# Gate and up projections: three matmuls of 256 columns a weight block against one of 512 and one of 256, with an addition on VectorE

## The chip, the cores and the metric

The kernel runs on one core of a Trainium2 chip. The metric is device microseconds of that core for one execution, 985.59 us as the median of three runs (983.49 to 986.75). The profile is one further execution of the same program.

## The reference, cut to what matters

Two transformer-like blocks run over 256 tokens of width 1024, in float32. The change touches the first half of both feed-forward parts:

```python
# first block
h = rmsnorm(x, ffn_pre_norm)
f = (silu(h @ w_ffn_gate) * (h @ w_ffn_up)) @ w_ffn_down
# second block: w_up has 2 * 2816 columns
u = h @ w_up
u = sum(pad(u)[:, j:j + t] * conv_w[j] for j in range(3)) + conv_b
a, g = split(u, 2)
f = (gelu(a) * g) @ w_down
```

d_ff is 2816, so that each of the two stages makes 22 pairs of output tiles of 128 features by 256 tokens, with 8 weight blocks of 128x128 to each tile.

## The kernel before, in words

**Numbers in two parts.** Every float32 operand of a projection is split into a high part (a cast to fp32r) and a low part (the value minus the high part). A product is three matmuls: high weight by high activation, high weight by low activation, low weight by high activation (PASSES, line 1488).

**The weight stream.** All weights come as one stream of 128x128 blocks. SP loads slots of 16 blocks (1 MB) into `raw`, which has three slots (line 477); before slot n it waits until the low parts of slot n-3 are made. Eight blocks are a unit. ScalarE casts a unit to `w_hi` (line 582), after PE has finished the unit four before. The low part `w_lo` of a unit is made by VectorE (line 975, even units) or GpSimd (line 545, odd units) as a tensor_tensor with `raw` and `w_hi` as inputs; in the first two fills of the gate and of the up stage VectorE makes all of them (`_DVE_ONLY`, line 90). PE waits for the low part at the first block of each unit (line 1496).

**A fill.** `pair` (line 1527) fills one PSUM bank of the ring `pj` (three banks): two tiles of 256 columns, 8 blocks each, 3 matmuls a block, so 48 matmuls and two units. The stages in question are `ff` (22 fills of gate and up of the first block) and `up` (22 fills of the second). `pe_step` counts finished fills and units.

**What follows a fill.** The engines run in the order of the program. For `ff` fill j, ScalarE: cast of unit 2j+4 (`split_target`, possible from the middle of the fill), wait for the end of the fill, cast of unit 2j+5 (`behind_target`), silu of the gate half (line 759), then the high part of product j-1 (line 762). VectorE: low part of unit 2j+4 (`feed_behind`, line 1201), product with the other half (line 1205), then the low part of product j-1 (`ff_lo`, line 1194). For `up` fill j, ScalarE: the two casts in the same way, two activations (line 929), gelu of j-1 (line 935), high part of product j-2 (line 938). VectorE: low part of unit 2j+4, wait for line 929, four scalar_tensor_tensor for the convolution (lines 1456 and 1463, one input in PSUM and one in SBUF), `ff_lo` of j-2 (line 1194), product of j-1 (line 1473, both inputs in SBUF). GpSimd makes the low part of unit 2j+5.

**What comes next.** `stream("down")` and `stream("down2")` (line 1570) take the activations `ff` as the stationary operand and four weight blocks (512 columns) as the moving one, into `acc` (four banks).

**Memory.** In SBUF, in this order: `raw` (24 KiB of each partition), `w_hi` and `w_lo` (16 KiB each), `x`, `y`, `sq` (8 KiB each), `h` (16 KiB, from 80 to 96 KiB, all high parts ahead of all low parts), constants and small buffers, and from about 120 KiB the arena, in which buffers of different stages share places: `ff` from its start (44 KiB), `merged_s` and `o_hg_s` at +32 KiB, `mix` at +35, `mem_n` at +51, `o_na` at +56, `o_ca` at +64. PSUM holds `pj` (banks 0 to 2), `acc` (3 to 6) and `st` (7).

Of the kernel before, what the change touches and what calls it, by code (L numbers as in the profile page):

```python
# [41 lines left out]
UB = 8  # L42
SBUF_WORDS = 52912
PJ = 3

# [22 lines left out]
RING = [n for n, f in enumerate(FILLS) if f[3] != "acc"]  # L68
INDEX = {(name, j): n for n, (name, j, _, _) in enumerate(FILLS)}
FIRST_BLOCK = [sum(f[2] for f in FILLS[:n]) for n in range(len(FILLS) + 1)]  # L70
NBLOCKS = FIRST_BLOCK[-1]
# [97 lines left out]
def program(nc, x_tok, mem_tok, pt, wstream, wproj, vecs, gains, consts, rope_tab, decay_tab, rpb, out, toep):  # L169
    ctx = ExitStack()  # L170
    with ctx:
# [18 lines left out]

        raw = place("raw", [RAW, 16, P])
        w_hi = place("w_hi", [UNITS, UB, P], R32)
        w_lo = place("w_lo", [UNITS, UB, P], R32)
        x = place("x", [2, D])
        y = place("y", [KT, S])
        sq = place("sq", [KT, S])
        h = place("h", [2, KT, S], R32)
        vec = place("vec", [NVEC])
# [11 lines left out]
        soft = place("soft", [2, 3, 2])  # L210
        arena = (top[0] + 127) // 128 * 128

        def at(kib, name, *shape, dt=F32):
            return place(name, list(shape), dt, offset=arena + int(1024 * kib))

# [55 lines left out]

        pj = [ctx.enter_context(nc.psum_tensor(f"pj{i}", [P, 2, S], F32)) for i in range(PJ)]
        acc = ctx.enter_context(nc.psum_tensor("acc", [P, 2, D], F32))
        sc = [acc[:, i // 2, 512 * (i % 2):512 * (i % 2) + 512] for i in range(4)]
        st = ctx.enter_context(nc.psum_tensor("st", [P, 512], F32))

# [19 lines left out]
        f_hi = sem("f_hi")  # L296
        up_full = sem("up_full")
        acc_done = sem("acc_done")
        mean_ready = sem("mean_ready")
# [75 lines left out]
        def bank(name, j):  # L375
            return pj[RING.index(fi(name, j)) % PJ]

# [191 lines left out]
        def _(act):  # L569
# [185 lines left out]
            for j in range(23):  # L755
                if j < 22:
                    wait_fill("ff", j)
                    wait_gate_slot(act, "ff", j)
                    A(gate_tmp[:, gate_slot("ff", j), 0], bank("ff", j)[:, 0], ACT.Silu).then_inc(gate_done, 1)  # L759
                if j:  # L760
                    wait_read(act, "ff", j - 1)
                    nc.scalar.copy(ff[:, 0, j - 1], prod_tmp[:, (j - 1) % 2]).then_inc(f_hi, 1)
# [160 lines left out]
            for j in range(24):  # L923
                if j < 22:
                    wait_fill("up", j)
                    if j >= 2:
                        act.wait_ge(up_full, j - 1)
                    for i in range(2):
                        ins = A(gate_tmp[:, j % 2, i], bank("up", j)[:, i], ACT.Identity,  # L929
                                bias=col("conv_b", 22 * i + j), scale=col("conv_w", 44 + 22 * i + j))  # L930
                    ins.then_inc(up_lin, 1)
# [14 lines left out]
        def _(dve):  # L946
# [248 lines left out]

            ff_lo.count = 0
            dve.wait_ge(toep_zero, 16)
            for j in range(23):
                if j < 22:
                    gates[0] += 1  # L1200
                    feed_behind("ff", j)
                    wait_gate(gates[0])
                    if j >= 2:
                        dve.wait_ge(ff_ready, j - 1)
                    V.tensor_tensor(prod_tmp[:, j % 2], bank("ff", j)[:, 1], gate_tmp[:, gate_slot("ff", j), 0],  # L1205
                                    ALU.mult).then_inc(freed["dve"], 1)
# [241 lines left out]
            for j in range(24):  # L1448
                if j < 22:
                    feed_behind("up", j)  # L1450
                    dve.wait_ge(up_lin, j + 1)
# [32 lines left out]
        def _(pe):  # L1484
# [21 lines left out]
            def open_fill(name, j):  # L1506
                n = fi(name, j)
                r = RING.index(n)
                if r >= PJ:
                    m = RING[r - PJ]  # L1510
                    who = FILLS[m][3]
                    pe.wait_ge(freed[who], freed_count(m, who))
                assert at_block[0] == FIRST_BLOCK[n] or FILLS[n][2] == 0
                return pj[r % PJ]

            def tile_out(dst, src, kts=KT, ready=None, turn=0):

                for n in range(kts):
# [4 lines left out]
                    for i, (a, b) in enumerate(PASSES):  # L1523
                        last = mm(dst, w[a], src[:, b, kt], start=n == 0 and i == 0, stop=n == kts - 1 and i == 2)  # L1524
                    step(last, at_block[0])

            def pair(name, j, src, kts=KT, ready=None, turn=0):
# [169 lines left out]
            for j in range(22):  # L1697
                pair("ff", j, h, ready=h_turned("wout"))

            def ff_kt(first):  # L1700
                def ready(i, tt):
                    if tt == 0:
                        pe.wait_ge(ff_ready, first + i + 1)
# [11 lines left out]

            stream("down", ff_part, FT, ff_kt(0), ahead_of={FT - 4 + 7: ("down", (0, 1))})
            stream("ple", h_part, KT, ple_ready, head=4, tail=2, ahead_of={3: ("down", (2, 3))})
# [180 lines left out]
            for j in range(22):  # L1898
                pair("up", j, h, ready=h_turned("wout2"))
            stream("down2", ff_part, FT, ff_kt(FT))  # L1900

# [123 lines left out]
```

## Time and profile before

| what | value |
|---|---|
| median of the runs | 985.59 us |
| the profiled execution, its own time | 984.05 us |
| its span, first to last instruction | 982.3 us |
| PE busy (matmul) | 947.2 us, 96% |
| weight loads busy | 888.0 us, 90% |
| VectorE, ScalarE, GpSimd busy | 624.7, 514.5, 325.7 us |
| share of PE in the chain that ended last | 83% |
| gate stage `ff`, first to last fill | 168.1 to 295.0 us |
| `up` stage | 785.3 to 913.7 us |
| granted TensorE clock, mean | 0.995 of 2.4 GHz |

The span is 1.75 us shorter than the execution's own time. Matmuls are pipelined and their ends are modelled, so the time of a run of matmuls is read from their starts, or from the chain of waits, and not from their busy time.

### The profile page before, as it was taken

How to read it: one execution, taken by the hardware profiler on the slowest of the kernel's cores; microseconds unless marked ns; L12 is line 12 of the kernel's file. 1: busy time of each engine (PE TensorE's matmuls, PEld its weight loads, DVE VectorE, ACT ScalarE, POOL GpSimd, SP SyncE). 2: the span in 40 equal slices, each digit the busy share in tenths (PEclk: the TensorE clock that was granted, in tenths of full speed). 3: DMA queues.
4: the chain of work that ended last, by engine and by line, in shares of the span. 5: the costliest groups of instructions: out<-in, count | busy, mean ns of one | idle time of the engine just before them, and what ended most of it. 6: DMA issues, size and time to landing. Idle time of an engine off the chain costs nothing.

```text
span 982.3 us, 16396 instructions
## 1 busy us (share of the span) xinstructions
PE 947.2 (96%) x6822; PEld 888.0 (90%) x6822; DVE 624.7 (64%) x842; ACT 514.5 (52%) x790; POOL 325.7 (33%) x136
## 2 busy tenths in 40 slices
PE   7999999999999999999999999999899899999997
PEld 7998986999998878999999998998799799999885
DVE  4998576566663257567598978865555545666522
ACT  6853475444444356555444445555445456666532
POOL 0000000334434400002564533555685124443441
PEclk9999999999999999999999999999999999999999
DMA  9652344655555454545524335333356445555551
GB/s 356 208 202 86 139 149 152 199 190 191 172 178 205 175 171 172 172 171 173 172 87 133 127 99 179 129 129 129 130 176 214 147 163 199 176 172 189 190 178 43
DMA packets 30441, 162.65 MB, mean 166 GB/s; under 512 B 9089, under 2 KB 9489, under 8 KB 11936
## 3 DMA queue, kind: packets, MB, share of 16 engines
q1 hardware_dynamic: 30304, 161.53, 48.1%
q8 instruction: 54, 0.88, 0.4%
q14 instruction: 19, 0.16, 0.0%
q0 software_dynamic: 64, 0.08, 0.0%
HBM read 160.48 MB, written 1.12 MB: 165 GB/s over the span
## 4 chain that ended last, share of the span: by engine, by line
PE 83%; DVE 9%; ACT 4%; issue 2%; DMA 2%; SPq 0%; DVEq 0%; ACTq 0%
PE pj L1524 52%; PE acc L1589 18%; PE pj L1542 5%; PE acc L1761 3%; DMA raw<-wstream 2%; PE acc L1624 1%; DVE w_lo L975 1%; ACT w_hi L582 1%; DVE y L1027 1%; ACT sq L588 1%; PE st L1624 1%; DVE ret_inv L1138 1%; DVE conv_y L1067 1%; PE acc L1838 0%; DVE h L1033 0%
## 5 line engine op out<-in xcount | busy, mean ns | idle before, releaser
L545 POOL TENSOR_TENSOR w_lo<-raw,w_hi 128x1024 fp32r<-128x1024 f32 x124 | 313.9, 2536 | 636.0 <-ACT w_hi L582 635.8
L1524 PE MATMUL pj<-h,w_hi 128*128 128x256 f32 x2816 | 512.3, 284 | 7.7 <-DVE h L1033 3.9
L582 ACT CAST w_hi<-raw 128x1024 fp32r<-128x1024 f32 x284 | 296.2, 1048 | 344.4 <-PE pj L1524 240.3
L1524 PEld LDWEIGHTS pj<-h,w_hi 128*128 128x128 f32 x2816 | 440.4, 192 | 11.1 <-issue 5.8
L1524 PE MATMUL pj<-h,w_lo 128*128 128x256 f32 x1408 | 399.0, 283 | 0.0
L975 DVE TENSOR_TENSOR w_lo<-raw,w_hi 128x1024 fp32r<-128x1024 f32 x160 | 201.8, 1270 | 126.2 <-ACT w_hi L582 116.1
L1524 PEld LDWEIGHTS pj<-h,w_lo 128*128 128x128 f32 x1408 | 270.8, 192 | 0.0
L1589 PE MATMUL acc<-w_hi,ff 128*128 128x512 f32 x352 | 96.1, 395 | 0.0
L1589 PEld LDWEIGHTS acc<-w_hi,ff 128*128 128x128 f32 x352 | 66.1, 188 | 15.2
L1589 PE MATMUL acc<-w_lo,ff 128*128 128x512 f32 x176 | 55.2, 395 | 0.0
L1194 DVE TENSOR_TENSOR ff<-prod_tmp,ff 128x256 fp32r<-128x256 f32 x44 | 53.6, 1221 | 0.9 <-ACT ff L938 0.9
L1456 DVE SCALAR_TENSOR_TENSOR gate_tmp<-pj,vec,gate_tmp 128x255 f32<-128x255 f32 x44 | 19.2, 478 | 48.3 <-ACT gate_tmp L929 48.3
L1542 PE MATMUL pj<-w_hi,h 128*128 128x256 f32 x256 | 46.9, 285 | 0.8 <-ACT v_ret L655 0.8
L1542 PEld LDWEIGHTS pj<-w_hi,h 128*128 128x128 f32 x256 | 40.0, 192 | 1.1 <-ACT v_ret L655 1.0
L1589 PEld LDWEIGHTS acc<-w_lo,ff 128*128 128x128 f32 x176 | 33.2, 188 | 7.7
L1205 DVE TENSOR_TENSOR prod_tmp<-pj,gate_tmp 128x256 f32<-128x256 f32 x22 | 9.3, 424 | 43.9 <-ACT gate_tmp L759 43.9
L1542 PE MATMUL pj<-w_lo,h 128*128 128x256 f32 x128 | 36.2, 283 | 0.0
L1290 DVE COPY_PREDICATED st_hg<-con,acc 128x256 f32<-128x256 int32 x56 | 21.9, 444 | 15.5 <-PE acc L1761 13.8
L1067 DVE SCALAR_TENSOR_TENSOR conv_y<-conv_in,vec,conv_y 128x256 f32<-128x256 f32 x74 | 31.2, 479 | 0.5
L1418 DVE TENSOR_TENSOR merged<-merged,prod_tmp 128x256 f32<-128x256 f32 x16 | 26.2, 1641 | 0.5
L1542 PEld LDWEIGHTS pj<-w_lo,h 128*128 128x128 f32 x128 | 24.5, 192 | 0.0
L1413 DVE SCALAR_TENSOR_TENSOR prod_tmp<-gate_tmp,pj 128x256 f32<-128x256 f32 x16 | 6.7, 420 | 26.5 <-ACT gate_tmp L907 26.5
(241 smaller groups left out, 1159.2 us busy)
## 6 DMA issues: line engine op xcount, KB each, us to landing
raw<-wstream SPq DMA_DIRECT2D x142, 1024.0 KB, 4.9
toep_t<-toep SPq DMA_DIRECT2D x16, 96.0 KB, 3.0
x<-x_tok SPq DMA_DIRECT2D x2, 512.0 KB, 5.0
mem<-mem_tok SPq DMA_DIRECT2D x1, 1024.0 KB, 12.1
w_ple<-wproj SPq DMA_DIRECT2D x1, 1024.0 KB, 7.1
out_t<-y SPq DMA_DIRECT2D x4, 256.0 KB, 2.3
decay<-decay_tab SPq DMA_DIRECT2D x1, 768.0 KB, 5.8
gain_mix_pre<-gains SPq DMA_DIRECT2D x1, 512.0 KB, 6.5
```

Source lines behind the costliest of these rows:

```text
L545: nc.gpsimd.tensor_tensor(w_lo[:, u % UNITS], unit_of_raw(u), as_f32(w_hi[:, u % UNITS]), ALU.subtract).then_inc(lo_ready["pool"], 1)
L582: nc.scalar.copy(w_hi[:, u % UNITS], unit_of_raw(u)).then_inc(hi_ready, 1)
L975: V.tensor_tensor(w_lo[:, u % UNITS], unit_of_raw(u), as_f32(w_hi[:, u % UNITS]), ALU.subtract).then_inc(lo_ready["dve"], 1)
L1067: ins = V.scalar_tensor_tensor(out=conv_y[:, j], in0=src, scalar=weight, in1=conv_y[:, j], op0=ALU.mult, op1=ALU.add)
L1194: V.tensor_tensor(ff[:, 1, j], prod_tmp[:, j % 2], as_f32(ff[:, 0, j]), ALU.subtract).then_inc(ff_ready, 1)
L1290: ins = V.copy_predicated(dst[:, 4 * a:4 * a + 4:3], m2, src)
L1418: ins = V.tensor_tensor(merged[:, j], merged[:, j], prod_tmp[:, i % 2], ALU.add)
L1524: last = mm(dst, w[a], src[:, b, kt], start=n == 0 and i == 0, stop=n == kts - 1 and i == 2)
L1542: last = mm(b[:, tt], src[:, xa, kt, tt * P:tt * P + P], ws[kt][wa], start=kt == 0 and i == 0, stop=kt == KT - 1 and i == 2)
L1589: last = mm(acc[:, tt, 512 * g:512 * g + 512], src(b, i, tt), w[:, u % UNITS, 4 * g:4 * g + 4].rearrange("p a b -> p (a b)"), start=i == 0 ...
L1624: last = mm(out, diag[:, w], conv_in[:, t, w:w + S], start=w == first, stop=w == end - 1)
L1761: last = mm(sc[g][:, c:c + P], tile(k_mix[g // 2], 2 * (g % 2) + a, tt), q, start=True, stop=True)
```

## The change

The two stages use a new helper `wide_pair`. For each weight block it issues one matmul of the high weight against high and low activations side by side (512 columns, into a whole bank) and one of the low weight against the high activations (256 columns, added to the first half of that bank). A fill now takes two banks, one for each tile, and alternates between banks 6, 7 (half of `acc`) and 0, 1. After the fill VectorE adds the two halves of both banks with one tensor_reduce over 128x1024 values into one bank (3 for even fills, 2 for odd), which the consumers then read. ScalarE waits for that sum.

```diff
+WIDE_BANKS = ((6, 7), (0, 1))
+SUM_BANKS = (PJ, 2)
...
-        raw = place("raw", [RAW, 16, P])
         w_hi = place("w_hi", [UNITS, UB, P], R32)
         w_lo = place("w_lo", [UNITS, UB, P], R32)
+        h_both = place("h", [KT, 2, S], R32)
+        h = h_both[:].rearrange("p k b s -> p b k s")
+        arena = (top[0] + 127) // 128 * 128
+        top[0] = arena + 1024 * ARENA_KIB
+        raw = place("raw", [RAW, 16, P])
         x = place("x", [2, D])
...
-        h = place("h", [2, KT, S], R32)
...
+        ring = ctx.enter_context(nc.psum_tensor("ring", [P, PJ + 1, 2, S], F32))
+        pj = [ring[:, i] for i in range(PJ)]
+        st = ring[:, PJ].rearrange("p a s -> p (a s)")
...
# ScalarE, in both stages
                 if j < 22:
                     wait_fill("ff", j)
+                    wait_summed(act, "ff", j)
...
# VectorE
+            def add_halves(name, j):
+                dve.wait_ge(pe_step, fill_step(fi(name, j)))
+                b = wide(name, j)
+                V.tensor_reduce(bank(name, j), b.rearrange("p i a s -> p i s a"), AX.X, ALU.add).then_inc(summed, 1)
...
+                    add_halves("ff", j)
                     feed_behind("ff", j)
...
+                    add_halves("up", j)
                     feed_behind("up", j)
...
# PE
             def open_fill(name, j):
                 n = fi(name, j)
-                r = RING.index(n)
-                if r >= PJ:
-                    m = RING[r - PJ]
-                    who = FILLS[m][3]
-                    pe.wait_ge(freed[who], freed_count(m, who))
+                for m in earlier_fills(n):
+                    if name in WIDE and FILLS[m][0] == name:
+                        wait_summed(pe, *FILLS[m][:2])
+                    else:
+                        pe.wait_ge(freed[FILLS[m][3]], freed_count(m, FILLS[m][3]))
...
+            def wide_pair(name, j, ready):
+                b = open_fill(name, j)
+                for i in range(2):
+                    both = b[:, i].rearrange("p a s -> p (a s)")
+                    for kt in range(KT):
+                        w = take()
+                        if i == 0 and j == 0:
+                            ready(kt)
+                        mm(both, w[0], h_both[:, kt].rearrange("p a s -> p (a s)"), start=kt == 0, stop=False)
+                        last = mm(b[:, i, 0], w[1], h[:, 0, kt], start=False, stop=kt == KT - 1)
+                        step(last, at_block[0])
...
             for j in range(22):
-                pair("ff", j, h, ready=h_turned("wout"))
+                wide_pair("ff", j, h_turned("wout"))
...
             for j in range(22):
-                pair("up", j, h, ready=h_turned("wout2"))
+                wide_pair("up", j, h_turned("wout2"))
```

`earlier_fills` names the last fills that used the same banks; within a stage PE waits before fill j for the sum of fill j-2. The down projections wait for the sum of fill 20 before they write the banks 6 and 7. In the new layout `w_hi`, `w_lo` and `h` lie below 48 KiB, the arena from 48 to 132 KiB, `raw` and the rest above it.

## Rows read from the trace of the kernel before

**Rows 1.** The page: busy time by engine, and the chain that ended last
```profile
PE 947.2 (96%) x6822; PEld 888.0 (90%) x6822; DVE 624.7 (64%) x842; ACT 514.5 (52%) x790; POOL 325.7 (33%) x136
...
PE 83%; DVE 9%; ACT 4%; issue 2%; DMA 2%; SPq 0%; DVEq 0%; ACTq 0%
PE pj L1524 52%; PE acc L1589 18%; PE pj L1542 5%; PE acc L1761 3%; DMA raw<-wstream 2%; PE acc L1624 1%; DVE w_lo L975 1%; ACT w_hi L582 1%; DVE y L1027 1%; ACT sq L588 1%; PE st L1624 1%; DVE ret_inv L1138 1%; DVE conv_y L1067 1%; PE acc L1838 0%; DVE h L1033 0%
```

**Rows 2.** The chain in order of time (start us, us, what, how many)
```profile
168.09 126.94 PE pj L1524 x1056
...
754.58 16.74 PE acc L1589 x72
785.31 128.44 PE pj L1524 x1056
913.75 61.35 PE acc L1589 x264
```

**Rows 3.** Busy time by stage: gate stage, then up stage
```profile
168.10:295.00 126.90, 126.90 (x1057) 126.90 (x1058) 76.70 (x64) 58.30 (x85) 50.48 (x21) 1.00 0.56 189
...
790.00:912.00 122.00, 122.00 (x1019) 122.00 (x1018) 73.31 (x143) 77.41 (x125) 50.79 (x21) 1.00 0.53 181
```

**Rows 4.** The chain from 368 to 378 us: `h` stationary, 512 moving columns
```profile
367.86 10.20 PE acc L1589 x45
```

**Rows 5.** VectorE's groups by shape, whole span
```profile
L1360 DVE TENSOR_REDUCE soft<-acc 128x2 f32<-128x512 f32 x4 | 2.7, 682 | 0.0
...
L1479 DVE TENSOR_TENSOR x<-x,acc 128x1024 f32<-128x1024 f32 x2 | 2.4, 1221 | 7.1 <-PE acc L1589 7.1
```

**Rows 6.** One up fill in order of time: last matmul, ScalarE's cast, VectorE, GpSimd
```profile
850.11 0.28 PE L1524 MATMUL pj<-h,w_lo 128*128 128x256 f32 x1
...
850.48 1.05 ACT L582 CAST w_hi<-raw 128x1024 fp32r<-128x1024 f32 x1 [1.83 <-PE pj L1524]
...
851.43 1.01 ACT L929 ACTIVATE gate_tmp<-pj,vec 128x256 f32<-128x256 f32 x2
851.61 2.42 POOL L545 TENSOR_TENSOR w_lo<-raw,w_hi 128x1024 fp32r<-128x1024 f32 x1 [3.34 <-ACT w_hi L582]
852.35 0.41 ACT L935 ACTIVATE gate_tmp<-gate_tmp 128x256 f32<-128x256 f32 x1
852.48 0.87 DVE L1456 SCALAR_TENSOR_TENSOR gate_tmp<-pj,vec,gate_tmp 128x255 f32<-128x255 f32 x2 [2.17 <-ACT gate_tmp L929]
852.65 0.40 ACT L938 CAST ff<-prod_tmp 128x256 fp32r<-128x256 f32 x1
...
854.18 0.41 DVE L1194 TENSOR_TENSOR ff<-prod_tmp,ff 128x256 fp32r<-128x256 f32 x1
854.51 0.42 DVE L1473 TENSOR_TENSOR prod_tmp<-gate_tmp 128x256 f32<-128x256 f32 x1
854.85 1.22 DVE L975 TENSOR_TENSOR w_lo<-raw,w_hi 128x1024 fp32r<-128x1024 f32 x1
```

**Rows 7.** One gate fill in order of time: GpSimd and VectorE
```profile
198.33 2.40 POOL L545 TENSOR_TENSOR w_lo<-raw,w_hi 128x1024 fp32r<-128x1024 f32 x1 [3.35 <-ACT w_hi L582]
198.57 0.42 DVE L1205 TENSOR_TENSOR prod_tmp<-pj,gate_tmp 128x256 f32<-128x256 f32 x1 [1.94 <-ACT gate_tmp L759]
198.91 2.10 DVE L1194 TENSOR_TENSOR ff<-prod_tmp,ff 128x256 fp32r<-128x256 f32 x1
```

**Rows 8.** Down projection in order of time: VectorE, then GpSimd
```profile
924.35 2.67 DVE L975 TENSOR_TENSOR w_lo<-raw,w_hi 128x1024 fp32r<-128x1024 f32 x1 [0.68 <-ACT w_hi L582]
...
926.07 3.22 POOL L545 TENSOR_TENSOR w_lo<-raw,w_hi 128x1024 fp32r<-128x1024 f32 x1
```

**Rows 9.** Near-simultaneous starts, in order of time: GpSimd, then VectorE
```profile
610.10 2.90 POOL L545 TENSOR_TENSOR w_lo<-raw,w_hi 128x1024 fp32r<-128x1024 f32 x1 [0.48 <-ACT w_hi L582]
...
610.10 0.68 DVE L989 TENSOR_TENSOR o_hg_s<-o_hg,o_hg_s 128x512 fp32r<-128x512 f32 x1
```

**Rows 10.** DMA: the weight slots, KB each, median us to landing
```profile
raw<-wstream SPq DMA_DIRECT2D x142, 1024.0 KB, 4.9
```

More of the change, by code:

```diff
@@ L43 @@
 SBUF_WORDS = 52912
+ARENA_KIB = 84
 PJ = 3
@@ L69, with filled_banks, read_banks, earlier_fills @@
 INDEX = {(name, j): n for n, (name, j, _, _) in enumerate(FILLS)}
+WIDE = ("ff", "up")
+WIDE_FILLS = [(name, j) for name, j, _, _ in FILLS if name in WIDE]
+WIDE_BANKS = ((6, 7), (0, 1))
+SUM_BANKS = (PJ, 2)
+def filled_banks(n):
+    name, j = FILLS[n][:2]
+    return WIDE_BANKS[j % 2] if name in WIDE else (RING.index(n) % PJ,)
+def read_banks(n):
+    name, j = FILLS[n][:2]
+    return (SUM_BANKS[j % 2],) if name in WIDE else filled_banks(n)
+def earlier_fills(n):
+    found = set()
+    for b in filled_banks(n):
+        before = [m for m in RING if m < n and b in filled_banks(m) + read_banks(m)]
+        found.update(before[-1:])
+    return sorted(found)
 FIRST_BLOCK = [sum(f[2] for f in FILLS[:n]) for n in range(len(FILLS) + 1)]
@@ L210, in program @@
         soft = place("soft", [2, 3, 2])
-        arena = (top[0] + 127) // 128 * 128
         def at(kib, name, *shape, dt=F32):
+            assert 1024 * kib + 4 * np.prod(shape) <= 1024 * ARENA_KIB, name
             return place(name, list(shape), dt, offset=arena + int(1024 * kib))
@@ L270, in program @@
         squares = gate_tmp[:].rearrange("p a b s -> p (a b s)")
-        pj = [ctx.enter_context(nc.psum_tensor(f"pj{i}", [P, 2, S], F32)) for i in range(PJ)]
+        ring = ctx.enter_context(nc.psum_tensor("ring", [P, PJ + 1, 2, S], F32))
+        pj = [ring[:, i] for i in range(PJ)]
+        st = ring[:, PJ].rearrange("p a s -> p (a s)")
         acc = ctx.enter_context(nc.psum_tensor("acc", [P, 2, D], F32))
+        acc4 = acc[:].rearrange("p t (b a s) -> p (t b) a s", b=2, a=2)
         sc = [acc[:, i // 2, 512 * (i % 2):512 * (i % 2) + 512] for i in range(4)]
-        st = ctx.enter_context(nc.psum_tensor("st", [P, 512], F32))
         mix_keys = sem("mix_keys")
@@ L297, in program @@
         up_full = sem("up_full")
+        summed = sem("summed")
         acc_done = sem("acc_done")
@@ L375, in bank, with wide, wait_summed @@
         def bank(name, j):
-            return pj[RING.index(fi(name, j)) % PJ]
+            return ring[:, read_banks(fi(name, j))[0]]
+        def wide(name, j):
+            a, b = filled_banks(fi(name, j))
+            return acc4[:, 2:4] if a == 6 else ring[:, a:b + 1]
+        def wait_summed(eng, name, j):
+            eng.wait_ge(summed, WIDE_FILLS.index((name, j)) + 1)
         def flat(b):
@@ L925, in _ @@
                     wait_fill("up", j)
+                    wait_summed(act, "up", j)
                     if j >= 2:
@@ L1507, in open_fill @@
                 n = fi(name, j)
-                r = RING.index(n)
-                if r >= PJ:
-                    m = RING[r - PJ]
-                    who = FILLS[m][3]
-                    pe.wait_ge(freed[who], freed_count(m, who))
+                for m in earlier_fills(n):
[3 more added lines that the diff above has]
+                        pe.wait_ge(freed[FILLS[m][3]], freed_count(m, FILLS[m][3]))
                 assert at_block[0] == FIRST_BLOCK[n] or FILLS[n][2] == 0
-                return pj[r % PJ]
+                return wide(name, j) if name in WIDE else pj[filled_banks(n)[0]]
             def tile_out(dst, src, kts=KT, ready=None, turn=0):
@@ L1697, in _, with ff_kt @@
             for j in range(22):
-                pair("ff", j, h, ready=h_turned("wout"))
-            def ff_kt(first):
+                wide_pair("ff", j, h_turned("wout"))
+            def ff_kt(first, wide_name):
                 def ready(i, tt):
+                    if i == 0 and tt == 1:
+                        wait_summed(pe, wide_name, 20)
                     if tt == 0:
@@ L1714, in ple_ready @@
                     wait_turned("down", 2 * tt + i // 4)
-            stream("down", ff_part, FT, ff_kt(0), ahead_of={FT - 4 + 7: ("down", (0, 1))})
+            stream("down", ff_part, FT, ff_kt(0, "ff"), ahead_of={FT - 4 + 7: ("down", (0, 1))})
             stream("ple", h_part, KT, ple_ready, head=4, tail=2, ahead_of={3: ("down", (2, 3))})
@@ L1898, in _ @@
             for j in range(22):
-                pair("up", j, h, ready=h_turned("wout2"))
-            stream("down2", ff_part, FT, ff_kt(FT))
+                wide_pair("up", j, h_turned("wout2"))
+            stream("down2", ff_part, FT, ff_kt(FT, "up"))
 def host_layout(inputs):
```

## The prediction

> **What bounds the kernel now.** I read the page first, for the engine that is full: PE is busy 96% of the span and carries 83% of the chain; the pairs' line 1524 alone has 52% [rows 1]. Then the chain in order of time: the gate stage is one unbroken piece of 126.94 us for its 1,056 matmuls, and the up stage one of 128.44 us [rows 2]. So both stages go at PE's pace: 126.94 / 1,056 = 120.2 ns a matmul, 5.77 us a fill (5.76 in steady state). The up stage is longer by 1.5 us; the change doesn't touch that. Third, the stage table: VectorE is busy 76.7 of 126.9 us in the gate stage and 73.3 of 122 us in the up stage [rows 3], that is 3.5 and 3.5 us of each 5.76 us fill. PE sets the time, and VectorE has 2.3 us to spare in each fill. The argument turns on whether the new addition fits there, and on when.
>
> **Part 1, the matmuls.** Each block loses two matmuls of 256 columns and gains one of 512. 256 columns take 120 ns where 2.4 GHz (granted clock 1.00 in both stages [rows 3]) needs 106.7: 13.3 ns for each matmul beside its columns. For 512 columns there are three rows: 45 in 10.20 us = 226.7 ns with `h` stationary [rows 4], 264 in 61.35 us = 232.4 ns with `ff`, and 72 in 16.74 us = 232.5 ns with `merged_s` [rows 2]. The nearest is 226.7, since it has the weights and `h` as operands and is again 13.3 ns over its columns. So a block costs 226.7 + 120 = 346.7 instead of 360 ns: 13.3 ns for 352 blocks = 4.7 us a stage, **9.4 us** in both; a fill takes 5.55 us. Bounds: at 240 ns (two matmuls of 256, nothing shared) the gain is 0; at 232.4 it is 5.4 us; at the bare 213.3 ns it is 18.8 us.
>
> The Trainium skill (TensorE: Matmul & The Clock Gate, Back-to-back issue gap) puts an isolated matmul at columns / 2.4 GHz + 2.5 ns. By that a block would go from 327.6 to 325.0 ns, and the change would bring 1.8 us in all. The 120 ns of this trace disagree with its 109, so the sum goes by the rows.
>
> **Part 2, the layout.** Streams whose activation buffer lies at 120 KiB and above take 232.4 ns, the one with `h` (80 to 96 KiB) 226.7 [rows 2, 4]. After the change `ff` lies at 48 to 92 KiB and `merged_s` at 80 to 96. If the place is the cause, 528 + 96 matmuls gain 5.7 ns each, 3.6 us; I take **3.1 us**, since nothing in the trace separates place from buffer and part of the other buffers moves too. Ends: 0 and 4 us. The move of `raw` to 132 KiB I cost at nothing: the slots land in 4.9 us [rows 10], less than a fill, and are needed over a fill later.
>
> **Part 3, the addition.** 44 tensor_reduce of 1,024 inputs and 512 outputs on VectorE. The nearest row has 512 inputs from PSUM, 682 ns; a 1,024 tensor_tensor with PSUM input takes 1,221 [rows 5]. 682 + 512 / 0.96 GHz = 1.22 us. Half as much isn't excluded by a row but would need two inputs a cycle; the upper end is 2.1 us, one more pass for the 512 outputs. 44 x 1.22 = 54 us of VectorE, all beside PE if the order works out.
>
> **Part 4, the order on VectorE.** Count from the start of the cast of the odd unit, which the end of a fill releases [rows 6] (at 850.48, 0.37 after the start of the last matmul). GpSimd's low part starts at 1.13 and ends at 3.55 [rows 6]. A VectorE instruction with two SBUF inputs and a GpSimd low part exclude each other: the 256-element `ff_lo` that started 0.58 after GpSimd took 2.10 instead of 0.41 us and ended 0.28 after it [rows 7, 6]; a low part that met GpSimd took 2.67, and GpSimd behind it 3.22 instead of 2.40 [rows 8, 7]. Instructions with one input in PSUM run through (0.42 during GpSimd [rows 7]; lines 1456 and 1463 alike [rows 6]).
>
> Now the addition comes first: 0 to 1.22. Behind it on VectorE stands the even unit's low part, made until now in mid-fill, when GpSimd was done. It starts at about 1.16 (successors start 0.07 early [rows 6]), against GpSimd's 1.13. **This is a race within 0.03 us.** At a tie in the trace VectorE got through (0.68 us) and GpSimd took 2.90 [rows 9]; at +0.58 it lost [rows 7].
>
> *VectorE first:* its low part ends at 2.4, GpSimd's at 4.65. In the up stage ScalarE waits for the sum until 1.25, its two activations end at 2.3, the convolution runs 2.3 to 4.0, `ff_lo` is blocked until 4.9, the product ends at 5.3: before the next fill's end at 5.55, with 0.3 to spare. PE needs the even low part at 5.55 and the odd one at 8.3. Nothing stalls. In the gate stage the work ends at 4.9.
>
> *GpSimd first:* the low part ends at 3.55 + 1.08 = 4.63. Gate stage: product and `ff_lo` until 5.3, still inside the fill, so 4.7 us are gained either way. Up stage: four convolution steps (1.70), `ff_lo` (0.33) and product (0.33 + 0.08) [rows 6] end at 7.0, past 5.55, see the first rival.
>
> PE waits for the sum of two fills before, at least 3 us old in either case. The DMA of a slot starts up to 1.3 us later and has over 3 us of slack. At the end of the gate stage the last high part comes some 4 us later on ScalarE (the addition, then a product behind a late low part), and with it the cast of the fifth unit of the down projection; that unit is needed 11 us after the stage, so it costs nothing.
>
> **Sum.** 984.05 (the profiled execution; span 982.3) - 9.4 - 3.1 = 971.6. The median is 1.54 above that execution, so 973.1: **973 us**.
>
> **Rivals.**
>
> *A. GpSimd wins the race, and the up stage falls behind: slower.* The product (two SBUF inputs) starts at 6.59, which is 1.04 of the next fill, 0.09 ahead of GpSimd's 1.13: GpSimd is held 0.19 (as rows 8 and 9 show), the low part ends 0.19 later, and a fill or two later the product comes behind GpSimd and is blocked itself. From then on PE waits for low parts. The loop over two fills: convolution, `ff_lo`, product 2.40; addition 1.21; ScalarE's activations, gelu, high part and two casts 2.67; GpSimd's start 1.13 and work 2.40; `ff_lo` and product behind it 0.27 + 0.28; addition 1.14; low part 1.22: 12.7 us for two fills, 6.36 each where 5.76 were. Five fills at 5.55 and sixteen at some 6.35 make +8.0 for the up stage, and the down projection after it starts on late low parts, +2.4. Sum: 984.05 - 4.7 + 8.0 + 2.4 - 3.1 = 986.7, or 988.2 against the median; each 0.1 us on the addition makes it 1.6 more. With 1.3 us, where GpSimd wins more surely, 989.7. It decides at an addition of some 1.2 us and ends at some 1.6, where the product falls behind GpSimd's end. For it: the arithmetic above. Against it: the tie of rows 9, and a race that I can't place to 0.03 us.
>
> The Trainium skill (SBUF — State Buffer, Who interferes with whom) has the same mechanism as a rule: a VectorE instruction with two SBUF inputs and a GpSimd one that reads SBUF share a port pair, and the one that issues first blocks the other for its whole length. Rows 7 and 8 agree. By "issues first" read to the letter, 1.13 is before 1.16 and rival A is the outcome.
>
> *B. The addition takes 1.6 to 2.1 us.* The up stage then has no blocked product but VectorE is nearly full: some 5.76 a fill, a gain of 1.9 less 1.2 of late low parts; 984.05 - 4.7 - 0.7 - 3.1 = 975.6, or 977 against the median. For it: strided reads from two banks and PSUM outputs, which no row shows.
>
> *C. The matmul of 512 gains nothing over two of 256* (the 13.3 ns go with the columns): only the layout's 3.1 is left, 982.5; and without that 985.6. Against it: rows 4. A milder case, 232.4 ns, gives 977.
>
> **Chances.** Forecast with VectorE first, 0.54; A 0.26; B 0.10; C 0.04; the milder case of C or something else in between 0.06. About 0.3%, 3 us, is what a measurement can tell from no change. A splits into 0.08 within 3 us and 0.18 above; C and a partial A give 0.07 more within; the others are faster: faster 0.66, same 0.15, slower 0.19. Range: the forecast with the layout's and the pitch's bounds reaches from 968 to 977, its own range; to leave out no more than 2 in 10 it has to reach through A: 968 to 989.5.
>
> **What would show it.** In the timeline of a gate fill: wide matmuls 227 ns apart to the next start, 5.55 us a fill, stage pieces of 122 and 124 us in the chain. TENSOR_REDUCE 128x512 at 1.22 us. In an up fill, VectorE's low part at 1.2 us when it won, above 3 us when it lost; the product at 0.42, or above 2 us in rival A, with PE waiting for `w_lo` of line 975. Down projections at 227 ns. The forecast is wrong if PE waits for VectorE in the up stage, if the addition is longer than 1.3 us, or if the 512 columns take over 232 ns.

## The result, and the profile after

| | before | changed |
|---|---|---|
| median of the runs | 986.17 us (983.49 to 987.03) | 976.36 us (973.71 to 977.04) |
| ratio to the kernel before | | 0.9906 (0.9889 to 0.9924) |
| the profiled execution | 984.05 us | 973.71 us |

The medians are of four executions each. Run again later on another occasion the changed kernel stood at 0.9917 (0.9891 to 0.9943). By these ratios it is 8 to 9 us faster (the two medians above are 9.8 apart). Forecast were 973 us and a gain of 12.5.

First the page of the changed kernel, its busy time and the shares of the chain:

```profile
PE 936.8 (96%) x6118; PEld 848.7 (87%) x6118; DVE 688.4 (71%) x886; ACT 518.2 (53%) x790; POOL 371.1 (38%) x136
...
PE 86%; DVE 8%; ACT 4%; issue 2%; DMA 1%; SPq 0%; DVEq 0%; ACTq 0%
PE ring L1579 28%; PE acc L1657 18%; PE acc L1591 9%; PE ring L1591 8%; PE ring L1610 5%; PE acc L1592 4%; PE ring L1592 4%; PE acc L1831 3%; PE acc L1692 1%; ACT w_hi L627 1%; DVE w_lo L1022 1%; DVE y L1074 1%; DMA gain_mix_pre<-gains 1%; PE ring L1692 1%; DVE ret_inv L1185 1%
```

PE has 704 instructions fewer and is still full. VectorE went up by 64 us and none of it shows: its share of the chain fell from 9 to 8% against [rows 1]. GpSimd's busy time rose by 45 us with the same 136 instructions; something holds it.

The chain in order of time (start us, us, what, how many), against [rows 2]:

```profile
291.78 58.54 PE acc L1657 x258
...
358.95 15.25 PE acc L1657 x66
...
750.47 19.08 PE acc L1657 x84
...
904.67 59.98 PE acc L1657 x264
```

The down projection of the second block takes 59.98 us for its 264 matmuls, 227.2 ns each (232.4 before), and starts at 904.67 instead of 913.75. At its end the changed kernel is 10.4 us ahead in these two executions, which both had a mean granted clock of 0.995.

The busy time by stage (gate, then up), against [rows 3]:

```profile
172.90:291.60 118.70, 118.70 (x674) 102.99 (x673) 100.82 (x83) 59.37 (x84) 72.23 (x21) 1.00 0.56 191
786.00:904.00 118.00, 118.00 (x682) 103.21 (x682) 107.65 (x164) 78.07 (x125) 72.47 (x21) 1.00 0.55 185
```

Each block has two matmuls now. The gate stage: 118.7 us / 674 x 2 = 352.2 ns a block; the up stage: 118.0 / 682 x 2 = 346.0. (A few matmul starts are rounded in at the edges; between the starts of two additions there are 5.65 us in the gate and 5.547 us in the up stage, 353 and 346.7 ns a block.) Before it was 360 ns in both. From its first matmul to the first of the down projection the gate stage took 124.4 us instead of 126.8, the up stage 123.7 instead of 128.3. So the up stage gained the forecast 4.7 us and the gate stage half of it. VectorE is 85% busy in the gate stage and 91% in the up stage.

One fill of the up stage in order of time (start us, us, engine, line, operation), against [rows 6]:

```profile
849.24 1.23 DVE L1248 TENSOR_REDUCE ring<-ring 128x512 f32<-128x1024 f32 x1 [0.30 <-PE ring L1592]
849.29 1.05 ACT L627 CAST w_hi<-raw 128x1024 fp32r<-128x1024 f32 x1 [1.72 <-PE ring L1592]
850.38 1.22 DVE L1022 TENSOR_TENSOR w_lo<-raw,w_hi 128x1024 fp32r<-128x1024 f32 x1
850.42 3.45 POOL L590 TENSOR_TENSOR w_lo<-raw,w_hi 128x1024 fp32r<-128x1024 f32 x1 [2.10 <-ACT w_hi L627]
850.51 1.02 ACT L976 ACTIVATE gate_tmp<-ring,vec 128x256 f32<-128x256 f32 x2 [0.16 <-DVE ring L1248]
...
851.56 0.87 DVE L1511 SCALAR_TENSOR_TENSOR gate_tmp<-ring,vec,gate_tmp 128x255 f32<-128x255 f32 x2
...
853.26 0.89 DVE L1241 TENSOR_TENSOR ff<-prod_tmp,ff 128x256 fp32r<-128x256 f32 x1
...
854.08 0.41 DVE L1528 TENSOR_TENSOR prod_tmp<-gate_tmp 128x256 f32<-128x256 f32 x1
854.78 1.23 DVE L1248 TENSOR_REDUCE ring<-acc 128x512 f32<-128x1024 f32 x1 [0.30 <-PE acc L1592]
```

The addition takes 1.23 us. VectorE's low part starts at 850.38 and runs 1.22 us undisturbed; GpSimd's starts 0.04 later and takes 3.45 us instead of 2.42. The race was won by 40 ns. That is where GpSimd's 45 us come from: 22 low parts in each stage, 44 times about 1.03. `ff_lo` is then held by GpSimd (0.89 instead of 0.41), the product ends at 854.49, and VectorE waits 0.30 us for the next fill to end. This 0.3 us a fill is all the slack that VectorE has left in the up stage.

### The profile page after: what moved, and what is told of

It is laid out like the page before. It is cut to its first block, busy times and chain, and to the rows that moved or that the text cites. A ratio compares the mean times of both kernels' runs of the same rounds, so it can differ in the third digit from the quotient of the medians.

```text
span 971.9 us, 15074 instructions
## 1 busy us (share of the span) xinstructions
PE 936.8 (96%) x6118; PEld 848.7 (87%) x6118; DVE 688.4 (71%) x886; ACT 518.2 (53%) x790; POOL 371.1 (38%) x136
## 4 chain that ended last, share of the span: by engine, by line
PE 86%; DVE 8%; ACT 4%; issue 2%; DMA 1%; SPq 0%; DVEq 0%; ACTq 0%
PE ring L1579 28%; PE acc L1657 18%; PE acc L1591 9%; PE ring L1591 8%; PE ring L1610 5%; PE acc L1592 4%; PE ring L1592 4%; PE acc L1831 3%; PE acc L1692 1%; ACT w_hi L627 1%; DVE w_lo L1022 1%; DVE y L1074 1%; DMA gain_mix_pre<-gains 1%; PE ring L1692 1%; DVE ret_inv L1185 1%
## 5 line engine op out<-in xcount | busy, mean ns | idle before, releaser
L1579 PE MATMUL ring<-h,w_hi 128*128 128x256 f32 x1408 | 257.4, 285 | 3.7 <-DVE w_lo L1022 1.8
L1579 PEld LDWEIGHTS ring<-h,w_hi 128*128 128x128 f32 x1408 | 219.7, 192 | 6.7 <-issue 3.1
L1579 PE MATMUL ring<-h,w_lo 128*128 128x256 f32 x704 | 199.1, 283 | 0.0
L1579 PEld LDWEIGHTS ring<-h,w_lo 128*128 128x128 f32 x704 | 135.0, 192 | 0.0
L1591 PE MATMUL acc<-h,w_hi 128*128 128x512 f32 x352 | 125.9, 400 | 2.9 <-DVE h L1080 2.9
L1591 PE MATMUL ring<-h,w_hi 128*128 128x512 f32 x352 | 124.2, 396 | 0.0
L1592 PE MATMUL acc<-h,w_lo 128*128 128x256 f32 x352 | 99.0, 281 | 0.0
L1592 PE MATMUL ring<-h,w_lo 128*128 128x256 f32 x352 | 98.2, 279 | 0.0
L1591 PEld LDWEIGHTS acc<-h,w_hi 128*128 128x128 f32 x352 | 66.9, 190 | 19.4 <-DVE h L1080 2.0
L1591 PEld LDWEIGHTS ring<-h,w_hi 128*128 128x128 f32 x352 | 66.1, 188 | 15.9
L1592 PEld LDWEIGHTS acc<-h,w_lo 128*128 128x128 f32 x352 | 67.0, 190 | 0.0
L1592 PEld LDWEIGHTS ring<-h,w_lo 128*128 128x128 f32 x352 | 66.3, 188 | 0.0
L1610 PE MATMUL ring<-w_hi,h 128*128 128x256 f32 x256 | 46.9, 285 | 0.8 <-ACT v_ret L700 0.8
```

Of the source, the lines that this page charges most:

```text
L1591: mm(both, w[0], h_both[:, kt].rearrange("p a s -> p (a s)"), start=kt == 0, stop=False)
L1592: last = mm(b[:, i, 0], w[1], h[:, 0, kt], start=False, stop=kt == KT - 1)
L1610: last = mm(b[:, tt], src[:, xa, kt, tt * P:tt * P + P], ws[kt][wa], start=kt == 0 and i == 0, stop=kt == KT - 1 and i == 2)
```

## The experiments

Each version was timed beside the kernel before, and one execution of each was profiled. Of the last two the profiled execution is the only one.

### The new layout alone

```diff
--- before
+++ layout alone
-        raw = place("raw", [RAW, 16, P])
         w_hi = place("w_hi", [UNITS, UB, P], R32)
         w_lo = place("w_lo", [UNITS, UB, P], R32)
+        h = place("h", [2, KT, S], R32)
+        arena = (top[0] + 127) // 128 * 128
+        top[0] = arena + 1024 * 84
+        raw = place("raw", [RAW, 16, P])
```

> The kernel before with the new SBUF order alone (weights, h and the arena low), fills still in 48 matmuls of 256 columns. Theory L (the place of the activation buffer sets the cadence of the 512-column streams): both down projections and the wout2 stream go at 227 ns a matmul instead of 232.4, the fills stay at 5.76 us, and the time is 3 us (2.5 to 3.6) under the kernel before, near 983. Rival P (the two cadences are states that a stream falls into, and the fewer matmuls ahead of it changed them): the down projections stay at 232.4 ns and the time stays within 1 us of the kernel before, 986.

Measured: 981.66 us, 0.9959 (0.9944 to 0.9974), so 4.0 us faster (2.6 to 5.5). The chain:

```profile
169.41 128.44 PE pj L1525 x1056
297.84 58.51 PE acc L1590 x258
...
756.59 19.08 PE acc L1590 x84
786.95 128.42 PE pj L1525 x1056
915.37 59.88 PE acc L1590 x264
```

The down projections go at 226.8 ns a matmul. The fills go as before: both stages took 128.4 us, as the up stage did before, and the 126.9 of the gate stage before differs by a stretch of low clock alone (last section). Something near 40% of the gain of the whole change (by the intervals between 30 and 60%) has nothing to do with matmuls of 512 columns in the fills.

### The wide matmuls with the old layout

```diff
--- changed
+++ wide, old layout
+        raw = place("raw", [RAW, 16, P])
         w_hi = place("w_hi", [UNITS, UB, P], R32)
         w_lo = place("w_lo", [UNITS, UB, P], R32)
-        h_both = place("h", [KT, 2, S], R32)
-        h = h_both[:].rearrange("p k b s -> p b k s")
-        arena = (top[0] + 127) // 128 * 128
-        top[0] = arena + 1024 * ARENA_KIB
-        raw = place("raw", [RAW, 16, P])
...
+        h_both = place("h", [KT, 2, S], R32)
+        h = h_both[:].rearrange("p k b s -> p b k s")
...
+        arena = (top[0] + 127) // 128 * 128
```

> The changed kernel with the old SBUF order (h still interleaved high and low). Theory L: the down projections are back at 232.4 ns, the gate and up fills take 5.55 to 5.65 us, the time is 3 us above the changed kernel, 979 to 980. Rival P: the down projections stay at 227 ns and the time is that of the changed kernel, 976.5. A third outcome, fills above 5.65 us, would mean that wide matmuls need h or the weights low.

Measured: 979.10 us, 0.9930 (0.9909 to 0.9950). Chain, then the stage table (gate, up):

```profile
293.47 59.96 PE acc L1656 x258
...
909.99 61.62 PE acc L1656 x264
```

```profile
175.00:290.00 115.00, 115.00 (x665) 100.57 (x664) 98.01 (x81) 58.74 (x84) 69.58 (x21) 1.00 0.56 193
790.00:905.00 115.00, 115.00 (x653) 99.81 (x652) 103.41 (x158) 75.28 (x119) 68.96 (x20) 1.00 0.53 180
```

The down projections are back at 232.4 ns and above. The two parts, 4.0 for the layout and 6.9 for the wide matmuls, make 10.9 against 8.2 to 9.3 for both; that is within their intervals, and no closer than that. And the gate stage is now the quick one (115 / 665 x 2 = 345.9 ns a block) and the up stage the slow one (352.2), the other way round than in the changed kernel. So the two cadences (a cadence is here the steady distance between the starts of matmuls) are not a property of a stage.

### A lost race

```diff
--- changed
+++ lost race, in both stages (the up stage shown)
...
                     add_halves("up", j)
+                    for c in range(132 + 6 * j, 138 + 6 * j):
+                        V.memset(nudge[:, c:c + 1], 1.0)
                     feed_behind("up", j)
```

> The changed kernel with six one-column memsets on VectorE between the addition and the low part, in both stages (about 0.2 us a fill), so that GpSimd's low part starts first. Theory R (rival A of the prediction: the order of the two low parts decides): gate fills stay at 5.65 us; in the up stage the low part takes about 3.5 us instead of 1.2, within a few fills the product of two SBUF inputs is blocked behind GpSimd as well, PE waits for w_lo, fills average 6.3 to 6.5 us, and the time is 988 to 994. Rival S (VectorE has a microsecond to spare and a lost race only moves its waits): up fills stay at 5.55 us and the time is within 1 us of the changed kernel, 976.5.

Measured: 989.49 us, 1.0032 (1.0012 to 1.0051): slower than the kernel before, and 11 to 13 us slower than the changed one, for memsets that move VectorE's low part by 0.11 us, from 0.04 ahead of GpSimd's to 0.07 behind it. Two fills of the up stage, VectorE and GpSimd:

```profile
864.62 1.22 DVE L1249 TENSOR_REDUCE ring<-acc 128x512 f32<-128x1024 f32 x1
...
865.86 1.21 DVE L1023 TENSOR_TENSOR w_lo<-raw,w_hi 128x1024 fp32r<-128x1024 f32 x1
...
868.68 0.42 DVE L1242 TENSOR_TENSOR ff<-prod_tmp,ff 128x256 fp32r<-128x256 f32 x1
869.01 0.42 DVE L1533 TENSOR_TENSOR prod_tmp<-gate_tmp 128x256 f32<-128x256 f32 x1
869.35 1.23 DVE L1249 TENSOR_REDUCE ring<-ring 128x512 f32<-128x1024 f32 x1
869.46 2.39 POOL L591 TENSOR_TENSOR w_lo<-raw,w_hi 128x1024 fp32r<-128x1024 f32 x1 [5.39 <-ACT w_hi L628]
...
870.59 2.35 DVE L1023 TENSOR_TENSOR w_lo<-raw,w_hi 128x1024 fp32r<-128x1024 f32 x1
...
874.55 2.45 DVE L1242 TENSOR_TENSOR ff<-prod_tmp,ff 128x256 fp32r<-128x256 f32 x1
...
877.26 1.22 DVE L1249 TENSOR_REDUCE ring<-acc 128x512 f32<-128x1024 f32 x1
```

The additions start at 864.62, 869.35 and then 877.26: 4.73 and 7.91 us apart, 12.64 for two fills. Rival A of the prediction had worked out 12.7. It grows as forecast: the low part is held first (3.43 us in the first fill), a few fills later the product or `ff_lo` (2.45 us above) behind GpSimd. The gate stage lost the race in every fill too (its low parts took 3.43 us) and kept 5.547 us a fill. So the order matters only where VectorE has no slack.

### The low part ahead of the addition

```diff
--- changed
+++ low part first, in both stages (the up stage shown)
...
+                    feed_fill("up", j)
                     add_halves("up", j)
                     feed_behind("up", j)
```

> The changed kernel with VectorE's low part of the even unit ahead of the addition, in mid-fill, as in the kernel before. Theory R: GpSimd isn't held any more (2.4 us instead of 3.4), the race is gone, and since PE sets the pace in both orders the time is the same within 1 us, 976.5; fills 5.55 and 5.65. Rival T (the addition late in its order costs something, because the mid-fill low part runs into the next addition and ScalarE's activations wait): up fills grow by 0.1 us or more and the time is 2 us or more longer.

Measured: 981.25 us, 0.9956 (0.9936 to 0.9975), 4 to 5 us slower than the changed kernel. Rival T was right. One fill of the up stage:

```profile
856.43 1.23 DVE L1248 TENSOR_REDUCE ring<-acc 128x512 f32<-128x1024 f32 x1
857.69 1.02 ACT L976 ACTIVATE gate_tmp<-ring,vec 128x256 f32<-128x256 f32 x2 [2.30 <-DVE ring L1248]
...
858.75 0.87 DVE L1513 SCALAR_TENSOR_TENSOR gate_tmp<-ring,vec,gate_tmp 128x255 f32<-128x255 f32 x2 [1.09 <-ACT gate_tmp L976]
...
861.11 1.22 DVE L1022 TENSOR_TENSOR w_lo<-raw,w_hi 128x1024 fp32r<-128x1024 f32 x1
...
862.25 1.22 DVE L1248 TENSOR_REDUCE ring<-ring 128x512 f32<-128x1024 f32 x1
```

Between the addition and the convolution VectorE waits 1.09 us for ScalarE's two activations, and there is nothing to do in that time. The low part comes behind the product instead, and VectorE's loop closes at 5.82 us a fill. In the changed kernel the low part fills exactly this wait. In the gate stage, with a shorter list, the same order keeps 5.547.

PE is not slowed at once. It keeps 5.55 us a fill and goes at 5.82 only in the last five, so that the up stage gets only 1.4 us longer by it. Meanwhile VectorE falls behind, and most of the price is paid in the down projection, which took 65.1 us from its first start to its last instead of 59.7. After its first 48 matmuls PE waits 3.7 us for a low part, and a stretch at a granted clock of 0.5 follows that idle time (918.6 to 922.0):

```profile
904.35 10.90 PE acc L1659 x48
915.25 1.27 ACT L672
916.74 0.94 ACT w_hi L627
917.70 1.24 DVE w_lo L1022
918.98 50.70 PE acc L1659 x216
```

### The changed kernel again

> The changed kernel once more, beside the next three on the same chip. Expected 0.991 of the kernel before, 976 to 977, and VectorE's low part first in all fills of both stages. One of the two stages, gate or up, at 5.65 us a fill (353.3 ns a block) and the other at 5.55 (346.7), or both at 5.55: the four profiles so far had 5.65 once in the gate stage and once in the up stage, so I expect it not to be fixed to a stage.

Measured: 975.41 us, 0.9917 (0.9891 to 0.9943). VectorE's low part came first in every fill. The stage table (gate, up):

```profile
172.90:291.60 118.70, 118.70 (x674) 102.91 (x673) 98.80 (x83) 59.36 (x84) 70.47 (x21) 1.00 0.55 190
786.00:904.00 118.00, 118.00 (x669) 102.30 (x668) 103.44 (x158) 76.38 (x120) 68.96 (x20) 1.00 0.53 183
```

Now both stages have the slow cadence: 669 matmuls in the 118 us of the up stage where the first profile had 682. The same program, on the same data, goes at 346.7 or at 353 ns a block, which makes 2.3 us a stage. I had not listed the outcome with both slow.

### Wide matmuls grouped

```diff
--- changed
+++ grouped (in wide_pair, for each tile i)
-                    for kt in range(KT):
-                        w = take()
-                        mm(both, w[0], h_both[:, kt]...)
-                        last = mm(b[:, i, 0], w[1], h[:, 0, kt]...)
+                    pe.wait_ge(hi_ready, u + 1)
+                    for kt in range(KT):
+                        mm(both, w_hi[:, u % UNITS, kt], h_both[:, kt]...)
+                    pe.wait_ge(lo_ready[LO_ENGINE[u]], lo_count(u, LO_ENGINE[u]))
+                    for kt in range(KT):
+                        last = mm(b[:, i, 0], w_lo[:, u % UNITS, kt], h[:, 0, kt]...)
```

> The changed kernel with the 8 wide matmuls of a unit first and its 8 matmuls of the low weights behind them; PE waits for the high part before the first and for the low part before the second group. Theory G (the 6.6 ns more a block in some stages come from the alternation of 512 and 256 columns): all fills take 5.55 us in both stages, and the time is 0 to 2.5 us under the changed kernel. Rival H (they are a state of the stream whatever the order): one stage is at 5.62 to 5.66 us again. The later need of the low part changes nothing, since nothing waits for it in the changed kernel.

Measured: 974.17 us, 0.9897 (0.9872 to 0.9922), beside 975.41 for the changed kernel in the same job; the intervals overlap. Both stages have 5.587 us between additions, 349.2 ns a block: neither 346.7 as theory G had it nor the 5.62 to 5.66 of rival H. The other profiles say the same. Seven stages with grouped matmuls ran at one pace throughout (in this version, the next and the two with the split addition), and all seven had 5.587. Nine with 512 and 256 by turns did so: four had 5.547 and five 5.653, either of them with and without a stretch of low clock inside. So the alternation does matter, grouping gives one middle value, and the clock is not what picks the cadence.

### Grouped, with the race lost

The memsets of the lost race put into the grouped version, in both stages:

```diff
--- grouped
+++ grouped, lost race (the up stage shown)
...
                     add_halves("up", j)
+                    for c in range(132 + 6 * j, 138 + 6 * j):
+                        V.memset(nudge[:, c:c + 1], 1.0)
                     feed_behind("up", j)
```

> The grouped order with the six memsets on VectorE that let GpSimd's low part start first. PE now needs a low part 1.8 us later than in the run with the memsets alone. Theory Loop (after the lost race the up stage goes at the loop between VectorE, ScalarE and GpSimd, 12.7 us for two fills, in which PE has no part): up fills still average 6.3 us, PE waits for w_lo before the second groups, and the time is within 3 us of the run with the memsets alone, 986 to 990. Rival Deadline (the fills are long because the low part is late for PE by less than a microsecond, and PE's wait then moves all that follows): 1.8 us of slack take the waits away, up fills go back to 5.55 us and the time to 976 to 978.

Measured: 989.76 us, 1.0047 (1.0027 to 1.0066). The additions of the up stage are 7.79 and 4.73 us apart, 12.53 for two fills. 1.8 us more of slack for PE changed next to nothing (12.53 against 12.64): the loop runs through VectorE, ScalarE and GpSimd alone, and rival Deadline is out.

### The gate stage alone

```diff
--- changed
+++ gate only
-WIDE = ("ff", "up")
+WIDE = ("ff",)
...
-                    wait_summed(act, "up", j)
...
-                    add_halves("up", j)
...
-                    if i == 0 and tt == 1:
+                    if i == 0 and tt == 1 and wide_name in WIDE:
...
-                wide_pair("up", j, h_turned("wout2"))
+                pair("up", j, h, ready=h_turned("wout2"))
```

> Wide matmuls and addition in the gate stage alone, the up stage as in the kernel before, new SBUF order. If the parts add up: layout 3 to 4 us, gate stage 2.4 (at 5.65 us a fill) to 4.7 (at 5.55), so 978 to 980.5, ratio 0.992 to 0.995, and the up stage's fills at 5.76 us. If the addition on VectorE had a price outside its stage, the time would be above 982.

Measured: 977.91 us, 0.9934 (0.9911 to 0.9957), 6.5 us faster than before, with 5.65 us a gate fill: 4.0 for the layout and 2.5 for the gate stage. The remaining 2 us or so come from the up stage.

### The addition in two halves

```diff
--- grouped
+++ addition split
-                dve.wait_ge(pe_step, fill_step(fi(name, j)))
                 b = wide(name, j)
-                V.tensor_reduce(bank(name, j), b.rearrange("p i a s -> p i s a"), AX.X, ALU.add).then_inc(summed, 1)
+                for i in range(2):
+                    dve.wait_ge(pe_step, unit_step(FIRST_BLOCK[fi(name, j)] // UB + i))
+                    ins = V.tensor_reduce(bank(name, j)[:, i], b[:, i].rearrange("p a s -> p s a"), AX.X, ALU.add)
+                ins.then_inc(summed, 1)
```

> The grouped version with the addition in two: the half of the first tile after its unit, in mid-fill, the second after the fill, about 0.7 us each. VectorE's low part then starts at about 0.6 of a fill where GpSimd starts at 1.18, so the race has half a microsecond instead of 0.04. Theory R: GpSimd is held to 2.9 us instead of 3.4, the low part takes 1.2 us in every fill, and since PE sets the pace the time is that of the grouped version within 1 us, 973 to 975. Rival: 0.15 us more work a fill on VectorE, whose first half can only start after the product, makes it late for the second half; then up fills grow above 5.6 us.

```diff
--- addition split
+++ addition split, six memsets (the up stage shown)
...
                     add_halves("up", j)
+                    for c in range(132 + 6 * j, 138 + 6 * j):
+                        V.memset(nudge[:, c:c + 1], 1.0)
                     feed_behind("up", j)
```

> The same with the six memsets between the addition and the low part, which cost the grouped version 15 us. Theory R (what they cost is the order of the two low parts, not their own time): the low part now starts at about 0.75, still ahead of GpSimd, and the time is within 1 us of the version without memsets, 973 to 976. Rival W (VectorE is so full that 0.1 us more a fill tips it): the up stage goes to 6.2 us a fill again and the time to 986 to 990.

Measured: 974.86 us, 0.9875 (0.9852 to 0.9898), and with the six memsets 973.19 us, 0.9858 (0.9838 to 0.9877). A fill of the first:

```profile
850.15 0.70 DVE L1249 TENSOR_REDUCE ring<-ring 128x256 f32<-128x512 f32 x1 [0.26 <-PE ring L1597]
850.76 1.22 DVE L1022 TENSOR_TENSOR w_lo<-raw,w_hi 128x1024 fp32r<-128x1024 f32 x1
851.34 2.91 POOL L590 TENSOR_TENSOR w_lo<-raw,w_hi 128x1024 fp32r<-128x1024 f32 x1 [2.68 <-ACT w_hi L627]
```

The low part starts 0.58 us ahead of GpSimd instead of 0.04 (0.47 with the memsets), and the memsets that cost 15 us in the grouped version cost nothing that can be measured. So it is the order they disturb and not the time they take.

### Where the buffers lie

Two more places for the kernel before, one execution each: weights and `h` low and the arena from 96 KiB; `h` and the arena low and the weight parts from 124 KiB.

```diff
--- layout alone
+++ arena from 96 KiB: raw, x, y and sq ahead of it
         h = place("h", [2, KT, S], R32)
-        arena = (top[0] + 127) // 128 * 128
-        top[0] = arena + 1024 * 84
         raw = place("raw", [RAW, 16, P])
         x = place("x", [2, D])
         y = place("y", [KT, S])
         sq = place("sq", [KT, S])
+        arena = (top[0] + 127) // 128 * 128
+        top[0] = arena + 1024 * 84
```

> The kernel before (no wide matmuls) with weights and h low as in the new order, but raw, x, y and sq between them and the arena, which so starts at 96 KiB: ff lies at 96 to 140 KiB. If it is the place of the activations above a border between 96 and 120 KiB that gives 232 ns, the down projections take 232 ns, or part of their matmuls do; if the border lies higher or weights and activations only have to be near each other, 227 ns. The time is 982 to 986.

```diff
--- layout alone
+++ weights from 124 KiB
-        w_hi = place("w_hi", [UNITS, UB, P], R32)
-        w_lo = place("w_lo", [UNITS, UB, P], R32)
         h = place("h", [2, KT, S], R32)
         arena = (top[0] + 127) // 128 * 128
         top[0] = arena + 1024 * 84
         raw = place("raw", [RAW, 16, P])
+        w_hi = place("w_hi", [UNITS, UB, P], R32)
+        w_lo = place("w_lo", [UNITS, UB, P], R32)
```

> The kernel before with h and the arena low (h 0 to 16 KiB, arena 16 to 100) and the weight parts high, at 124 to 156 KiB. If only the place of the activations counts, the down projections take 227 ns and all fills 120 ns flat, time 982. If one of the two operands above the border is enough, all streams, the 256-column fills too, show the uneven cadence (115 to 122 ns, 232 ns for 512 columns), time 984 to 987.

Measured: 982.06 and 979.54 us. The chain of the first (arena from 96 KiB):

```profile
167.41 128.40 PE pj L1525 x1056
295.81 58.51 PE acc L1590 x258
...
786.25 126.95 PE pj L1525 x1056
913.20 59.88 PE acc L1590 x264
```

Neither brought 232 ns back: 58.51 us for 258 matmuls with `ff` up to 140 KiB, and the same with the weights at 124 to 156 KiB. "Low" is not what helps. One thing sets the old layout apart from all the quick ones, by the sizes in the source: its arena starts behind the small buffers, 128 bytes further from a multiple of 1 KiB than `h` and the weights; in the four quick ones all operands of PE share their offset. That fits every profile here and was not tried by itself, so it stays a guess.

## Why the prediction was right, and where it was off

- **What bounds the kernel** was right: PE set the pace before and sets it after, and 54 us of additions on VectorE cost nothing.
- **Part 1, the matmuls, is the term that was mis-sized.** It put a block at 346.7 ns, the row of 512-column matmuls [rows 4] plus 120 ns, and the gain at 4.7 us a stage. 346.7 is one of two cadences; 353 is the other, and three of the four stages in the two profiles of the changed kernel had it. That is 2.3 to 2.4 us a stage instead of 4.7. The rows that the sum used are streams of equal matmuls, and no row of before had 512 and 256 columns by turns; the range's 232.4 ns (5.4 us in both) covered it, the value taken didn't. In the quick cadence the total fits, but not its two parts, and that is luck: from the start of a wide matmul to the next start the mean is 231.8 ns (up stage of the first profile) and not 227, and from a 256-column one 114.9 and not 120. In the slow cadence they are 236.7 and 116.7 (its gate stage), so the prediction's own sign, 512 columns over 232 ns, came up there. The rule of the Trainium skill cited beside it (TensorE: Matmul & The Clock Gate, Back-to-back issue gap: 2.5 ns over the columns, by the estimate there 1.8 us in all) was further off.
- **Part 2, the layout:** 3.1 forecast, 4.0 (2.6 to 5.5) measured alone. The size was about right, and two steps under it were not. It left out one stream: the first output projection, 96 matmuls with `mix`, went from 233.2 to 227.6 ns as well. With it the changed kernel's profile gains 1.4 us in each down projection and 0.5 in each of the two output projections, 3.8 in all. And the cause given, the place in SBUF at 120 KiB and above, was not it: two other places, one with the activations and one with the weights high, are as quick.
- **Part 3, the addition:** 1.22 forecast, 1.23 measured. Strided reads from two banks and results in PSUM added nothing to the estimate; rival B is out.
- **Part 4, the order on VectorE:** the forecast put GpSimd's start 0.03 us ahead and took VectorE as the winner on the tie in [rows 9]. In the profile VectorE starts 0.04 ahead, because the addition starts some 0.05 us sooner than ScalarE's cast though both wait for the same end of a fill (849.24 against 849.29, and 0.053 to 0.055 in 43 of the profile's 44 fills); the estimate had them start together. The winner was named rightly, by a margin that the estimate could not see. VectorE's low part came first in all 44 fills of each of the two profiles. From there the times of the prediction hold to 0.1 us, counted from the start of the addition: low part to 2.36, GpSimd to 4.63, `ff_lo` to 4.9, product to 5.25.
- **Rival A** was the right mechanism for a lost race, with its price: 12.7 us for two fills worked out, 12.64 measured; 988.2 to 989.7 us worked out, 989.49 measured. It was given 0.26 and needed 0.04 us more. Its parts came out a little longer than worked out: the up stage took 137.0 us instead of 128.3 before (8.7 more against 8.0, where the prediction's own terms, five fills at 5.55 and sixteen at 6.35, make 8.4), and the down projection 4.4 us more than in the changed kernel against 2.4, with a stretch of low clock in it (931.7 to 935.1). The rule of the Trainium skill cited for it (SBUF — State Buffer, Who interferes with whom), that the instruction that issues first holds the other for its whole length, the traces bear out in both directions.
- **In the sum:** in the profiled pair, 984.05 less 2.3 (gate stage), 4.6 (up stage) and 3.8 (layout) is 973.4, and 973.71 was measured. Between the medians, 973 was forecast against 976.4. Two stages at 2.4 instead of 4.7 make +4.6, the layout 0.9 the other way: 976.7. That fits, but it takes the slow cadence for both stages of executions that have no trace, and these had a lower mean clock too (0.990 to 0.993 against 0.995). How the 3.4 us divide between the two is not shown.

## What to carry to other kernels

When an engine that has slack on average gets new work, write down its whole fill in order of time with the waits of the others in it: the addition was free only because the low part behind it filled a 1.1 us wait for ScalarE, and because it reached a lock of two engines 40 ns ahead. A margin like that is no design; split the work that stands ahead of the lock (0.7 us instead of 1.2 here) and look at the lead again. And time a change of places by itself: 4 of the 9 us came from the layout.

## What the runs showed of the hardware that was not expected

- Streams of matmuls settled in a steady cadence and stayed in it for a whole stage. 512 columns: 227 or 232.4 ns by the layout. 512 and 256 by turns: 346.7 or 353 ns for the two, in the same program and from one execution to the next. What picks one is open.
- The same 1,056 matmuls of a stage took 126.95 us or 128.4 to 128.44 us (both in the last fence above), the kernel unchanged between its two stages. A stretch at a granted clock of 0.5, that is 1.2 GHz, lies at the start of every one of the five longer ones (785.6 to 789.0 us in the kernel before, after PE had waited 1.77 us for `h`) and in none of the four shorter ones, so it costs 1.5 us. Executions of one program differ in the number of such stretches and so in their mean clock. Of the layout alone, twelve executions went from 984.23 us at 0.989 to 979.41 at 0.997 and 978.51 at 0.996. That is as much as most of the differences between the versions here: read a difference of 1 to 3 us with both clocks beside it.
- VectorE's instructions with an input in PSUM (the addition, the convolution steps) ran at full speed while GpSimd's low part was under way. Those with two inputs in SBUF (`w_lo`, `ff_lo`, product) did so only where they had started ahead of it; otherwise they ended behind it (`ff_lo` 0.89 instead of 0.41 us, `w_lo` 2.35 instead of 1.22).
